# Attention in a hybrid diffusion backbone: the softmax weights' transposes one quarter tile later, the products with v and the norm's sums two quarters later

## The reference, cut to what matters

```python
def block(qi):
    s = jnp.einsum('bqhcd,bkhcd->bhcqk', qi, k).astype(jnp.float32) * scale
    p = jax.nn.softmax(s, axis=-1)
    a = p[:, :, 0] - lam * p[:, :, 1]
    return jnp.einsum('bhqk,bkhe->bqhe', a.astype(v.dtype), v)
...
o = rmsnorm(o, subln_g) * (1 - lam_init)
pool_out = multiscale_pool(xpool, pool_w, pool_scale)
out = jnp.concatenate([o.reshape(b, n, DA_V_W), pool_out], axis=-1) @ w_out
```

## Time and profile before

| what | value |
|---|---|
| median of 3 runs | 2189.38 us |
| lowest, highest | 2186.27, 2192.53 us |
| profiled execution, first to last instruction (span) | 2179.9 us |
| TensorE busy | 1991.0 us, 91% |
| mean granted TensorE clock, as a share of full speed | 0.959 |
| attention stage, its entries from `rotq` 0 to g_ready at 8 | 105.1 to 336.9 us |

### The profile page before, as it was taken

The page is one execution under the profiler, slowest core; times in us unless marked ns, Lnnn a source line. Parts: engine busy times, 40 slices in busy tenths (PEclk is TensorE's granted clock), DMA queues, the critical chain, the costliest instruction groups (busy, mean ns, idle before and its releaser), DMA issues. The chain is left out here.

```text
span 2179.9 us, 33056 instructions
## 1 busy us (share of the span) xinstructions
PE 1991.0 (91%) x12945; PEld 1864.4 (86%) x12945; DVE 1154.7 (53%) x1505; ACT 670.4 (31%) x1093; POOL 1152.3 (53%) x437
## 2 busy tenths in 40 slices
PE   5789887989999999998999999997697999999997
PEld 3678776878899889997998999896696999999997
DVE  4655575667634653354647676768614452452353
ACT  4334332233211320121356464647201220120121
POOL 3233323535567556776454444440474777777763
PEclk8899988989999999999999999998798999999999
DMA  8211116524434522224143333322321222222221
GB/s 275 100 45 53 36 34 209 183 92 144 151 110 124 155 87 68 74 59 128 39 120 116 97 106 97 101 75 87 107 68 48 68 73 72 77 67 78 68 63 73
DMA packets 292913, 208.60 MB, mean 96 GB/s; under 512 B 7344, under 2 KB 284885, under 8 KB 292309
## 3 DMA queue, kind: packets, MB, share of 16 engines
q1 hardware_dynamic: 292821, 207.32, 31.2%
HBM read 196.63 MB, written 10.67 MB: 95 GB/s over the span
## 5 line engine op out<-in xcount | busy, mean ns | idle before, releaser
L828 POOL TENSOR_SCALAR w_hi<-raw 128x1024 fp32r<-128x1024 f32 (+1 forms) x216 | 629.7, 2915 | 983.5 <-PE ps L859 909.8
L859 PE MATMUL ps<-h_hi,w_hi 128*128 128x322 f32 (+1 forms) x2304 | 559.9, 324 | 22.3 <-DVE h_lo L1702 22.0
L859 PE MATMUL ps<-h_lo,w_hi 128*128 128x322 f32 (+1 forms) x2304 | 533.8, 313 | 0.0
L859 PE MATMUL ps<-h_hi,w_lo 128*128 128x322 f32 (+1 forms) x2304 | 533.1, 313 | 0.0
L831 POOL TENSOR_TENSOR w_lo<-raw,w_hi 128x1024 fp32r<-128x1024 f32 (+1 forms) x216 | 522.2, 2418 | 18.0
L859 PEld LDWEIGHTS ps<-h_hi,w_hi 128*128 128x128 f32 x2304 | 391.2, 192 | 51.0 <-issue 33.4
L859 PEld LDWEIGHTS ps<-h_hi,w_lo 128*128 128x128 f32 x2304 | 394.5, 191 | 0.0
L859 PEld LDWEIGHTS ps<-h_lo,w_hi 128*128 128x128 f32 x2304 | 391.5, 191 | 0.0
L859 PE MATMUL ps<-g_hi,w_hi 128*128 128x322 f32 (+1 forms) x816 | 190.4, 315 | 10.3 <-DVE g_lo L1956 10.3
L859 PE MATMUL ps<-g_lo,w_hi 128*128 128x322 f32 (+1 forms) x816 | 188.7, 313 | 0.0
L859 PE MATMUL ps<-g_hi,w_lo 128*128 128x322 f32 (+1 forms) x816 | 188.2, 312 | 0.0
(11 more groups left out here) (295 smaller groups left out, 2533.2 us busy)
## 6 DMA issues: line engine op xcount, KB each, us to landing
ada<-in_ada_w SPq DMA_DIRECT2D x48, 1024.0 KB, 5.3
raw<-in_ffn_w_up SPq DMA_DIRECT2D x88, 512.0 KB, 3.9
raw<-in_ssd_w_in SPq DMA_DIRECT2D x40, 512.0 KB, 4.1
R<-scr_acs SPq DMA_DIRECT2D x40, 512.0 KB, 4.8
raw<-in_ffn_w_down SPq DMA_DIRECT2D x32, 512.0 KB, 3.8
raw<-in_att_w_in SPq DMA_DIRECT2D x16, 512.0 KB, 6.1
raw<-in_ssd_w_out SPq DMA_DIRECT2D x16, 512.0 KB, 4.0
raw<-in_ffn_w_down SPq DMA_DIRECT2D x16, 384.0 KB, 3.4
```

The lines of the kernel that those rows point to most:

```text
L828: nc.gpsimd.tensor_scalar(w_hi[j % 2][:, 0:k, :], raw[j][:, 0:k, :], 1.0, None, ALU.mult).then_inc(w_hi_done, 1)
L859: ins = mm(out[:, cols], w[slot][:, k, :], x[:, k_of(k), cols], start=first and k == 0 and i == 0, stop=last and k == n - 1 and i == 2)
```

## The change

In the list, `T` of every chunk comes one quarter later (i = 5 + 2j for 4 + 2j), `PV` two quarters later (7 + 2j for 5 + 2j), `ssO` and `rbO` two quarters later. `S` and `mix` stay. For head 3 this carries `PV` of chunk 4 and `ssO` behind the last quarter of tile 15, among the `out` entries. Every instruction remains; only the order changes.

```diff
@@ def att_schedule():
-            at(4 + 2 * j, "T", h, j)
-            at(5 + 2 * j, "PV", h, j)
-        at(14, "ssO", h)
-        at(16, "rbO", h)
+            at(5 + 2 * j, "T", h, j)
+            at(7 + 2 * j, "PV", h, j)
+        at(16, "ssO", h)
+        at(18, "rbO", h)
...
-    after[(15, 3)] = after.get((15, 3), []) + [("out", 0), ("out", 1)] + after.pop((16, 0)) + [("out", 2), ("pool", 3)]
+    after[(15, 3)] = after.get((15, 3), []) + [("out", 0)] + after.pop((16, 0)) + [("out", 1)] + after.pop((16, 2)) + \
+        [("out", 2), ("pool", 3)]
```

## The result

| | before | changed |
|---|---|---|
| median of 11 runs | 2187.45 us | 2195.73 us |
| lowest, highest | 2179.93, 2192.53 us | 2188.14, 2200.24 us |
| ratio, 95% interval | 1 | 1.0036 [1.0021, 1.0052] |
| span of the profiled execution | 2179.9 us | 2197.1 us |

The account below looks back on a forecast made before the run. TensorE, busy 91% of the span, was taken as the bound, so only its stalls and half clock mattered, with VectorE bounding the stage's end. Terms 3.2 - 1.4 + 0.2 - 2.1 - 6.0 + 5.5 = -0.6, taken as -1: 2188.4 us, range 2182 to 2197.

Parts of the forecast that it names:

- (a) to (c): Heads: scores wait for copy of `T` ahead, +3.2 us; rotation stall shorter, -1.4; later `ssO` and `rbO`, +0.2.
- (d): `PV` of chunk 4 and `ssO` of head 3 move behind tile 15, into TensorE's idle time: -2.1 us.
- (e): Tile 12's end to tile 15's end: stalls of 10.0 us replace 16.0, -6.0 us, with ends -8.2 and -3.6.
- if L1801 is held after all: Lower end of (e), pool work 0's subtraction held beside GpSimd's L831: gain of only 3.6 us.
- (f): End of stage, pool work 3's end to `g_ready`: 8.5 us at full clock, 10.6 at half; +5.5, lower end +3.4.
- the gain in (e) lost: Rival, tile 12 to tile 15: L1801 loses its margin ahead of L831, waits only change places; 2190.8 us, chance 0.2.
- the clock against: Rival: TensorE falls to half clock behind remaining stalls of 2.4 to 3.5 us; up to 2198 us, chance 0.10.
- The rule on the port: Rival, pool work 0: first addition held inside GpSimd's L828 too, pushing L1801 behind L831; 2193 us, chance 0.03.

Follow-up runs that it names:

- three stalls filled: 28 extra matmuls nobody reads put into each of the three rotation stalls, in both kernels: 1.0009 for the changed kernel, 0.9983 for before.
- seven: Extra matmuls in the three rotation stalls and four more stalls, in both kernels: 0.9950 for before, 0.9964 for the changed kernel.
- tail put back, filled: Changed kernel with head 3's last `PV`, `ssO` and `rbO` back at their old entries, and extra matmuls in the three rotation stalls: 0.9993.
- subtraction left out: Changed kernel without the 128-column subtraction of pool work 0 (that part of the output not computed): 0.9998 of before.
- filled: Beside the subtraction left out: changed kernel without pool work 0's 128-column subtraction, with extra matmuls in the three rotation stalls: 0.9983.
- the two mixed kernels: Before with head 3's `T` and `PV` later, its last `PV` at entry 14, head 2's norm late: 1.0004; also with pooling copies on ScalarE: 0.9991.

## Why the prediction was wrong, point by point

(a) to (c), **the waits of heads 0 to 2: right in kind, too large in size.** The short `S` waits 0.42 us, not 0.74, full ones nothing that counts, `rbO` 0.93 and 0.92 for the 1.1 forecast. The rotation waits 3.06 us, not 2.8, since the held instruction is now the product ahead of the copy. The sum was +2.0; the heads differ by 0.7 us with three stalls filled and by 0.0 with seven, where the rotation stalls themselves are filled alike in both.

(d) **The work that leaves the path** does leave it. Where it was put back (tail put back, filled), VectorE waited 3.17 us for it, and 3.9 us were lost ahead of pool work 3, for the 2.1 forecast.

(e) **The step that failed.** "Stalls 10.0 for 16.0", 52.7 us from tile 12's end to tile 15's, for 58.7. Measured: 60.1. It failed twice.
First, the hold. The prediction gave L1801, the first of pool work 0's two subtractions, 0.4 us ahead of GpSimd's L831, and did not look at the second, 0.2 us behind it. The first (L1802 here) did begin ahead, by 0.14 us, and was not held. GpSimd came at tile 12's end + 3.20 us, not + 3.4, since its L829 took 2.77 us, not the 2.93 of the earlier trace rows. The second (L1803) began 0.07 us too late and was held. Where the last subtraction begins ahead, the stretch takes 52.5 us (subtraction left out: 263.84 to 316.34; filled: 257.30 to 309.82), so the sum of pieces came out, in part by luck: the waits there were 8.3 us (filled), not 10.0. With the hold and the clock held it is 54.9, where the prediction's own lower end, "if L1801 is held after all", says 55.1.
Second, and larger, the comparison itself: before's 58.7 contained half clock behind its two long stalls, while the 10.0 us of new stalls were counted at full clock. The named waits of the changed kernel do add up to 10.1 us (3.02, 0.56 where `rbO` was to wait 1.6, 2.88, 2.82 and 0.77). Before with its stalls filled takes 55.5 us. At equal clock the order gains 0.6 us here, not 6; and the changed kernel paid another 5.2 us (60.1 less 54.9) for half clock behind its stalls of 3.0 and 2.8 us, before 3.2 (58.7 less 55.5). In the second pair of profiles the stretch takes 60.1 us in before and 60.0 in the changed kernel.

(f) **The end of the stage: right.** 10.8 us against 10.6 forecast at half clock, and 8.4 against the 8.5 forecast at full clock, when the stall ahead of `rbO` is filled:

```profile
323.55 0.83 DVE L1875 TENSOR_TENSOR o_diag<-consts,small 128x640 f32<-128x640 f32 x1
...
324.53 0.46 PE L907 MATMUL ps<-o_diag,ones 128*128 128x128 f32 x2 [0.41 <-DVE o_diag L1875]
...
330.44 0.83 DVE L1896 TENSOR_TENSOR g_lo<-pmul,g_hi 128x642 fp32r<-128x642 f32 x1 [0.81 <-ACT g_hi L1430]
```

So 3.3 of the 5.7 us are the longer chain and 2.4 the clock.

**The rivals.** Two came true at once: the gain in (e) lost (0.2) and the clock against (0.10), the latter in milder form. They were priced as if they excluded each other, at 2190.8 and 2198, and the result lies between. The argument against the clock, "the stalls get shorter", was no argument: 3.0 us were enough to lose it. The rule on the port, in the form that L829 too would hold pool work 0 for 2 us, did not come true: L1793 took 0.91 us inside L829 (266.79, L829 from 265.95). But the prediction's reading that L828 does not agree with the rule was drawn from one row that began late inside it. In before `g_lo` of pool 0, begun 0.13 us behind L828, took 1.59 us instead of 0.83:

```profile
286.79 2.77 POOL L828 TENSOR_SCALAR w_hi<-raw 128x1024 fp32r<-128x1024 f32 x1 [17.24 <-PE ps L859]
286.92 1.59 DVE L1888 TENSOR_TENSOR g_lo<-pmul,g_hi 128x642 fp32r<-128x642 f32 x1 [0.81 <-ACT g_hi L1422]
```

That is a hold up to 0.89 us behind L828's start. L1793, begun 0.84 us behind L829, was held 0.05 us, to the same 0.89; L1792 of before, begun 1.26 us behind L828, was not held. So this operation of GpSimd holds VectorE for its first 0.9 us, and the rule above, the port for the whole instruction, does not fit it. It fits L832, which holds VectorE for nearly all of its 2.4 us (L1803, 268.87 + 2.88 - 0.69: until 2.3 us behind L832's start).

**The account.** The changed kernel is 8 us slower: by the profiles about 3 are the order (3.3 behind pool work 3, 0.6 won ahead of it), and about 5 are left for TensorE's clock, which it loses in more places. The ratios give the latter as 15.8 us won by filling in the changed kernel against 10.9 in before; this difference of 4.9 has an uncertainty of about 6, and rests on the profiles for its places. Shown are those behind head 3's `rbO` (2.4 us) and behind head 2's `ssO` and head 3's `PV`, low in both profiles of the changed kernel.

**What stays open:** why the clock falls behind a rotation in one execution and not in another. In the unfilled profiles it fell behind all twelve rotations with the changed order of heads 0 to 3, behind all three with `T` alone put back, and behind ten of fifteen with before's order up to there: four of nine in before, its second profile and the kernel with head 3 alone changed, but all six in the two mixed kernels. It differs between executions, so the order does not fix it; that the order makes it likelier is suggested by these counts, not shown.

## What to carry to other kernels

Before adding up what a shorter stall gives, write beside each stretch the clock at which it ran, and compare sums at the same clock; this kernel replaced two stalls of 5.7 and 5.4 us by three of some 3 us and one of 5, and the clock was low behind three of these four. Where TensorE had to wait some 3 us, matmuls into unused columns kept the clock and made before faster: 0.17% for three stalls, 0.50% for seven. They must end with the stall: where it shrank, they delayed the work behind them by 1.3 us. A margin of 0.4 us, worked out on paper between a VectorE instruction and a GpSimd one that can hold it, was none: cost both outcomes, with what each drags along, and look at every instruction of the group, not only the first.

## What the hardware showed that was not expected

Behind a rotation stall of 3.05 to 3.27 us the clock was low in 25 of 30 cases, and the same place could fall either way (0.50 or 1.00 behind 2.78 us, 2.9 us apart on the chain). Added work made before faster by 11 us and the changed kernel by 16. Leaving out an instruction of 0.29 us moved the time by 8 us, through 0.2 us of order between two engines and the clock that came with it; with the clock held it was worth 2.4. One operation of GpSimd (`w_hi`, 2.8 us) holds VectorE for its first 0.9 us, the other (`w_lo`, 2.4 us) for nearly its whole length.
